# GpSimd in place of VectorE for the gain product of the second token block at the end of the expert stage

## The chip, the core and the metric

The kernel is one program on one core of a Trainium2 chip. The core has TensorE (matrix products into PSUM, abbreviated PE; PEld is its loading of weights), VectorE (DVE), ScalarE (ACT), GpSimd (POOL), SyncE (SP), which issues most DMAs, and 16 DMA engines. All engines run their own instruction lists in order and wait for one another by semaphores. The metric is the time of one execution on the device in microseconds (us); smaller is better.

## What is computed

256 tokens of 1024 features (f32) go through two transformer blocks. The first has a chunkwise mLSTM beside sliding-window attention, cross attention to a memory of 256 rows, and a mixture with product keys (PEER): for each token and each of 8 heads 16 of 16384 experts, each a row of `expert_down` and one of `expert_up`. The second has gated linear attention beside block attention, an MLP of width 4096 and a gated addition of per-layer features. The change lies where the one passes into the other:

```python
def rmsnorm(x, g):
    xf = x.astype(jnp.float32)
    y = xf * lax.rsqrt(jnp.mean(xf * xf, axis=-1, keepdims=True) + EPS)
    return (y * g.astype(jnp.float32)).astype(x.dtype)
...
def first_block(...):
    ...
        h = h + peer_ffn(rmsnorm(h, g_ffn[l]), w_pq[l], sub_keys1[l], sub_keys2[l],
                         expert_down[l], expert_up[l])
    return rmsnorm(h, g_final)
...
def second_block(x, ...):
    ...
        h = rms_norm(x, norm_mix[i])
        u = h @ w_in[i]
        (gq, gk, gv, g_lr, g_r, mq, mk, mv, gate_a, gate_b) = jnp.split(u, points, axis=-1)
```

So the residual stream h after the experts is normed with `g_final`, which gives the second block's input x, and x is normed once more with `norm_mix` and multiplied with the weights `w_in`.

## The kernel before

**Tiling.** The tokens are two blocks of 128 (tb = 0, 1), one token in each of the 128 partitions. `X[:, tb, :]` is the residual stream, 128x1024 f32. Weights come as halves of 128x2048 f32 in a fixed order (`HALVES`) into a ring of three buffers. Each half is cut into two parts for the matrix products: ScalarE copies it rounded into the first tensor of a pair hl (L1439), and VectorE subtracts that from the ring's tile into the second (L2006, one instruction of 2.29 us with two SBUF inputs). On both engines `split_to(n)` does this for all halves up to number n that aren't done. TensorE makes three products for each pair of tiles (L817).

**The expert stage.** 256 indirect DMAs of GpSimd (L781) each gather, for one expert slot of one token block, the down row and the up row of the expert of each of the 128 tokens, into one of 8 buffers. VectorE multiplies and sums the down half of a gathered buffer with the normed tokens XG (L2490, two SBUF inputs of 128x1024), ScalarE applies the gelu (L1695), VectorE the gate (L2498), ScalarE makes a diagonal of the coefficients (L1702) and TensorE adds diagonal times up half to the accumulators in PSUM (L1169). Its last product is semaphore `pe["ex", 255]`. In GpSimd's list a wait for it and two memsets of the scan mask `scanm` (L786, L788) stand behind the gathers; the only reader of the mask is the scan of VectorE at L2529.

**The seam to the second block**, for each token block: VectorE adds the two accumulators to X (`residual_sum`, L2424, semaphore h3). It multiplies X by the factors of `g_final`, which lie in all partitions of GB, into HG (`gain_sum`, L2429, semaphore hgs); HG is the tile XG, whose reader, the expert stage, is done with that block by then. ScalarE squares and sums X (`final_sum`, L1718) and HG (`final_gained`, L1722). From the two sums come both norms: VectorE makes the variances (`final_var`, L2434 to L2437), ScalarE the root (`sqrt`, L1456), VectorE the inverse roots and a diagonal matrix `xdg` with their product (`final_root`, L2442 to L2449). TensorE multiplies HG with this diagonal, which turns and scales it (`turn_block`, L1157, waits for hgs and for the diagonal), ScalarE and VectorE copy the result in two parts to XT (`final_turned`, L1729, L2460), and VectorE writes the plain final norm back to X (`final_scale`, L2452).

For tb = 0 these steps are spread over the last 16 gathers of the second token block. For tb = 1 they stand behind all of them, woven with the halves n to n+3 of the weights of gv (n is the number of gv's first half). VectorE's order there is: split n, `residual_sum(1)`, `gain_sum(1)`, split n+1, `final_var(1)`, `final_root(1)`, split n+2, `final_turned(1)`, `final_scale(1)`. ScalarE's is: splits to n+1, `final_sum(1)`, `final_gained(1)`, two fetches (one loads other factors into GB), split n+2, the root, `final_turned(1)`. TensorE's is: 12 products with half n and 12 with half n+1 for token block 0, the two `turn_block(1, k)`, then 36 more products, the first 12 with half n+2.

Of the kernel before, what the change touches and what calls it, by code (L numbers as in the profile page):

```python
# [11 lines left out]
ALU = mybir.AluOpType  # L12
# [54 lines left out]
def program(nc, A, out):  # L67
    ctx = ExitStack()
    with ctx:
        def sb(name, shape, dt=F32):  # L70
            return ctx.enter_context(nc.sbuf_tensor(name, shape, dt))

        def count(name, keys, by=1):
            return Count(ctx.enter_context(nc.semaphore(name)), keys, by)

        def landed(name):
            return (ctx.enter_context(nc.semaphore(name)), 16)
# [3 lines left out]
        X = sb("X", [128, 2, 1024])  # L81
# [6 lines left out]
        GB = sb("GB", [128, 1024])  # L88
# [94 lines left out]
        HG = XG  # L183
# [51 lines left out]
        for j in range(4):  # L235
# [14 lines left out]
        at = {n: landed(f"c_{n}") for n in ("x0", "x1", "gains", "convw", "convb", "bif", "sinks", "gmh", "sk", "thin",  # L250
                                            "mem", "gb2", "bqk", "gffn", "gfin", "ggn", "gw2", "pT", "wple")}
# [106 lines left out]
        h3 = count("h3", [(tb, h) for tb in range(2) for h in range(2)])  # L358
        hgs = count("hgs", range(2))
# [349 lines left out]
        @block.sync  # L709
        def _(e):  # L710
            for tb in range(2):
                e.dma_start(X[:, tb, :], A["x"][tb * 128:tb * 128 + 128, :]).then_inc(at[f"x{tb}"][0], 16)
            for n, (name, k, h) in enumerate(HALVES):
                if (name, k, h) == ("xv", 0, 0):
                    e.dma_start(PWB[:, :], A["wple"]).then_inc(at["wple"][0], 16)
                    e.dma_start(pT[:, :, :], A["pT"]).then_inc(at["pT"][0], 16)
                if name == "ple":
                    continue
                if n >= RING:
                    e.wait_ge(*lo[n - RING])  # L720
                if n in (NUM["gv", 0, 0], NUM["gv", 0, 1]):
                    e.wait_ge(*gath[254 + n - NUM["gv", 0, 0]])
                e.dma_start(ring[:, n % RING, :], A["wt"][FIRST[name] + 2 * k + h]).then_inc(ld[n][0], 16)
            for k, tb, o, n in LAST:
                c = slice(k * 512 + o, k * 512 + o + n)
                e.wait_ge(*pgo[k, tb, o, n])
                e.dma_start(out[tb * 128:tb * 128 + 128, c], SG[:, tb, c]).then_inc(outs.sem, 16)
            e.wait_ge(*outs[4])


        @block.gpsimd
        def _(e):
            e.memset(ident[:, :], 0.0).then_inc(gstep.sem)
            e.memset(epsc[:, :], EPS)
            e.memset(sel[:, :, :], 0.0)
            e.memset(M1[:, :], 0.0)
            e.memset(CT[:, :], 0.0)
            e.memset(ones[:, :], 1.0)
            e.memset(cmask[:, :], 1.0).then_inc(gstep.sem)
            e.wait_ge(*gstep[0])  # L740
            e.affine_select(out=ident[:, :], in_=ident[:, :], compare_op=ALU.not_equal, fill=1.0, base=0,
                            pattern=[[-1, 128]], channel_multiplier=1).then_inc(const.sem)
            e.wait_ge(*gstep[1])
            e.affine_select(out=sel[:, :, :], in_=sel[:, :, :], compare_op=ALU.not_equal, fill=1.0, base=0,
                            pattern=[[-1, 4], [0, 128]], channel_multiplier=1)
            e.affine_select(out=M1[:, 0:128], in_=M1[:, 0:128], compare_op=ALU.is_gt, fill=NEG, base=0,
                            pattern=[[1, 128]], channel_multiplier=-1)
            e.affine_select(out=M1[:, 128:256], in_=M1[:, 128:256], compare_op=ALU.is_ge, fill=NEG, base=0,
                            pattern=[[-1, 128]], channel_multiplier=1)
            e.affine_select(out=CT[:, :], in_=CT[:, :], compare_op=ALU.is_ge, fill=-NEG, base=0,  # L750
                            pattern=[[1, 128]], channel_multiplier=-1)
            e.iota(ioi, pattern=[[1, 256]], base=-128, channel_multiplier=-1).then_inc(gstep.sem)
            e.wait_ge(*gstep[2])
            e.tensor_copy(DD[:, :], ioi).then_inc(gstep.sem)
            e.wait_ge(*gstep[3])
            e.affine_select(out=DD[:, :], in_=DD[:, :], compare_op=ALU.is_ge, fill=NEG, base=128,
                            pattern=[[-1, 256]], channel_multiplier=1)
            e.iota(ioi[:, 0:16], pattern=[[1, 16]], base=0, channel_multiplier=0).then_inc(gstep.sem)
            e.wait_ge(*gstep[4])
            e.tensor_copy(iot[:, :], ioi[:, 0:16]).then_inc(gstep.sem)  # L760
            e.wait_ge(*gstep[5])
            e.affine_select(out=cmask[0:64, :], in_=cmask[0:64, :], compare_op=ALU.is_ge, fill=0.0, base=0,
                            pattern=[[1, 64]], channel_multiplier=-1).then_inc(gstep.sem)
            e.wait_ge(*gstep[6])
            e.affine_select(out=cmask[64:128, :], in_=cmask[64:128, :], compare_op=ALU.is_ge, fill=0.0, base=0,
                            pattern=[[1, 64]], channel_multiplier=-1).then_inc(const.sem)

            e.wait_ge(*pe["XV", 3])
            for i in range(256):
                h, tb, s = i // 32, i // 16 % 2, 16 * (i // 32) + i % 16  # L770
                if i == 0:
                    e.wait_ge(*idx[0, 0, 0])
                if i == 8 or i % 16 == 0 and i > 0:
                    e.wait_ge(*idx[h, tb])
                if i == 2:
                    e.wait_ge(*pe["xo", 1, 1])
                if i == 6:
                    e.wait_ge(*pe["pq", 0, 1])
                if i >= NG:
                    e.wait_ge(*pe["ex", i - NG])  # L780
                e.indirect_dma_start(out=rows[i % NG][:, :], out_offset=None, in_=A["ex"],  # L781
                                     in_offset=bass.IndirectOffsetOnAxis(ap=eidx[:, tb, s:s + 1], axis=0)
                                     ).then_inc(gath[i][0], 16)

            e.wait_ge(*pe["ex", 255])
            e.memset(scanm, 1.0).then_inc(scan1.sem)  # L786
            e.wait_ge(*scan1[0])
            e.memset(scanm.rearrange("p (a b) -> p a b", b=64)[:, :, 0:1], 0.0).then_inc(scan1.sem)  # L788
# [3 lines left out]
        def _(e):  # L792
# [608 lines left out]
            for h in range(2):  # L1401
                n = NUM["pg", 1, h]
                e.wait_ge(*lo[n])
                w = [p[:, :].rearrange("p (k n) -> p k n", k=4) for p in PARTS[n]]
                for i, (_, tb, o, c) in enumerate(LAST[2:]):
                    ps = bank(("pg", 1, i)) if h == 0 else ps_of(("pg", 1, i))
                    m = prod(ps[:, 0:c], lambda a, k: XT[a][:, k, tb * 128:tb * 128 + 128],
                             lambda b, k: w[b][:, k % 4, o:o + c], range(4 * h, 4 * h + 4), h == 0, h == 1)
                    if h:
                        mark(m, ("pg", 1, i))  # L1410
                if h == 0:
                    mark(m, ("used", n))
# [572 lines left out]
        def _(e):  # L1985
# [13 lines left out]
            def split_to(n):  # L1999

                while parted[0] <= min(n, len(HALVES) - 1):
                    i = parted[0]
                    parted[0] += 1
                    e.wait_ge(*hi[i])
                    w = PARTS[i]
                    e.tensor_tensor(w[1][:, :], loaded(i), w[0][:, :].bitcast(F32),  # L2006
                                    ALU.subtract).then_inc(lo.sem)
# [412 lines left out]
            def residual_sum(tb):  # L2420
                e.wait_ge(*pe["ex", 239 + 16 * tb])
                for h in range(2):
                    x = X[:, tb, h * 512:h * 512 + 512]
                    e.tensor_tensor(x, ps_of(("acc", tb, h))[:, :], x, ALU.add).then_inc(h3.sem)  # L2424

            def gain_sum(tb):
                e.wait_ge(*at["gfin"])
                e.wait_ge(*h3[tb, 1])
                e.tensor_tensor(HG[:, tb, :], X[:, tb, :], GB[:, :], ALU.mult).then_inc(hgs.sem)  # L2429
# [84 lines left out]
            n = NUM["gv", 0, 0]  # L2514
            split_to(n)
            residual_sum(1)
            gain_sum(1)
            split_to(n + 1)
            final_var(1)
            final_root(1)  # L2520
# [286 lines left out]
```

## Time and profile before

| what | value |
| --- | --- |
| median of 3 runs | 1406.13 us (1404.08 to 1406.48) |
| the profiled execution | 1404.8 us |
| its span, first to last instruction | 1403.0 us |
| TensorE busy | 1265.9 us (90%) |
| VectorE busy | 947.8 us (68%) |
| ScalarE busy | 585.7 us (42%) |
| GpSimd busy | 273.8 us (20%) |

A page of the profile gives one execution. Times are counted from the start of the span. A timeline row has the start in us, the busy time in us, the engine, the line of the kernel, the operation, the tiles written and read (without buffer numbers: B is any of the working tiles, HG, the row buffers and the scan mask among them; st is a tile of small sums), the shapes and the number of instructions that the row merges. In brackets stands how long the engine had been idle before, and what ended this. The chain that ended last is followed backwards from the last instruction, each step to what released it. Of the engines' busy times the highest share isn't the answer by itself: what counts at one place is which wait ends last there.

### The profile page before, as it was taken

Reading aid. Unit: us, or ns where it says so; the run is one execution under the profiler, and the core shown is the slowest. Engines: PE = TensorE matmul, PEld = TensorE weight load, DVE = VectorE, ACT = ScalarE, POOL = GpSimd, SP = SyncE. Lnnn points to the kernel's source line nnn. Section 1 sums busy time; section 2 is a strip of 40 time slices with the busy share of each in tenths; the row PEclk is TensorE's granted clock in tenths of the full one; section 3 lists DMA queues with packets and bytes.
Section 4 is the critical chain, followed back from the end, with each engine's and each line's share of the span. In section 5 each row is a group of like instructions: output and inputs, shape, how many; then the busy total and the mean of one; then the engine's idle time right before and its main releaser. Section 6 shows DMA issues by size and latency. Waiting matters only on the chain.

```text
span 1403.0 us, 15322 instructions
## 1 busy us (share of the span) xinstructions
PE 1265.9 (90%) x5502; PEld 869.3 (62%) x5502; DVE 947.8 (68%) x1973; ACT 585.7 (42%) x1045; POOL 273.8 (20%) x281
## 2 busy tenths in 40 slices
PE   8999998988788878878787779899999999999998
PEld 8888897544243333424343234388688878888887
DVE  5657656877777777777777776655765556877445
ACT  4657453322223232222322223565556644555334
POOL 1000001443334344343434345100000000000000
PEclk9999998799999999999999999999999999999999
DMA  7443533999999999999999999845354445455551
GB/s 285 169 169 111 183 113 145 413 421 421 421 421 421 421 422 418 422 410 421 419 422 421 421 415 413 337 163 196 121 180 150 150 155 186 170 193 197 184 205 61
DMA packets 57123, 398.73 MB, mean 284 GB/s; under 512 B 7112, under 2 KB 7624, under 8 KB 9176
## 3 DMA queue, kind: packets, MB, share of 16 engines
q0 software_dynamic: 36864, 268.45, 46.2%
q1 hardware_dynamic: 18144, 126.10, 25.1%
q10 hardware_dynamic: 2040, 3.19, 0.7%
q8 instruction: 45, 0.74, 0.2%
q14 instruction: 30, 0.25, 0.0%
HBM read 396.67 MB, written 1.05 MB: 283 GB/s over the span
## 4 chain that ended last, share of the span: by engine, by line
PE 56%; DMA 24%; DVE 8%; ACT 7%; issue 3%; POOL 0%; ACTq 0%; SPq 0%; DVEq 0%; POOLq 0%
PE ps L817 35%; DMA B<-in_ex,eidx 23%; PE ps L1169 10%; PE ps L845 4%; DVE B L2490 3%; ACT hl L1439 3%; PE ps L846 2%; DVE hl L2006 2%; ACT diags L1702 1%; DMA ring<-in_wt 1%; ACT av_ L1695 1%; ACT L1695 1%; ACT L1691 1%; PE ps L1067 0%; PE ps L1049 0%
## 5 line engine op out<-in xcount | busy, mean ns | idle before, releaser
L1169 PE MATMUL ps<-B,diags 128*128 128x512 f32 x1024 | 487.9, 622 | 114.7 <-ACT diags L1702 114.7
L1169 PEld LDWEIGHTS ps<-B,diags 128*128 128x128 f32 x1024 | 191.3, 196 | 382.2 <-issue 197.0
L2490 DVE CUSTOM_DVE_ANT_0 B<-B 128x1024 f32<-128x1024 f32 x256 | 311.4, 1221 | 118.5 <-DMA B<-in_ex,eidx 118.4
L781 POOL DMA_INDIRECT B<-in_ex,eidx x256 | 267.7, 1046 | 611.8 <-PE ps L1169 363.8
L2006 DVE TENSOR_TENSOR hl<-ring,hl 128x2048 fp32r<-128x2048 f32 x115 | 263.2, 2290 | 180.0 <-ACT hl L1439 179.7
L1439 ACT ACTIVATE hl<-ring 128x2048 fp32r<-128x2048 f32 x115 | 219.8, 1912 | 117.5 <-PE ps L817 116.0
L817 PE MATMUL ps<-hl,R 128*128 128x512 f32 x936 | 218.2, 392 | 0.3 <-DVE R L2022 0.3
L817 PE MATMUL ps<-hl,XT 128*128 128x512 f32 (+1 forms) x888 | 203.6, 387 | 2.9 <-DVE hl L2006 2.4
L1695 ACT ACTIVATE av_<-av_ 128x2 f32<-128x2 f32 x128 | 26.0, 203 | 426.5 <-DVE av_ L2490 426.4
L817 PEld LDWEIGHTS ps<-hl,R 128*128 128x128 f32 x936 | 174.2, 188 | 36.8 <-DVE R L2022 0.7
L817 PEld LDWEIGHTS ps<-hl,XT 128*128 128x128 f32 x888 | 162.4, 188 | 38.6 <-DVE hl L2006 3.7
L817 PE MATMUL ps<-XT,hl 128*128 128x256 f32 x960 | 133.7, 297 | 2.9 <-DVE XT L2015 2.9
L817 PEld LDWEIGHTS ps<-XT,hl 128*128 128x128 f32 x960 | 120.9, 193 | 17.0 <-issue 16.4
L1702 ACT ACTIVATE diags<-ident,av_ 128x128 f32<-128x128 f32 x256 | 88.8, 394 | 29.1 <-DVE av_ L2498 29.1
L845 PE MATMUL ps<-XT,hl 128*128 128x512 f32 x256 | 89.1, 392 | 0.0
L846 PE MATMUL ps<-XT,hl 128*128 128x256 f32 x256 | 71.7, 280 | 0.0
L845 PEld LDWEIGHTS ps<-XT,hl 128*128 128x128 f32 x256 | 47.9, 187 | 10.8 <-DVE XT L2015 0.3
L2498 DVE TENSOR_TENSOR av_<-av_,gw 128x2 f32<-128x2 f32 x128 | 20.7, 162 | 43.9 <-ACT av_ L1695 43.8
L846 PEld LDWEIGHTS ps<-XT,hl 128*128 128x128 f32 x256 | 48.4, 189 | 0.0
L1959 ACT ACTIVATE B<-ps 128x256 f32<-128x256 f32 x32 | 10.5, 381 | 37.2 <-PE ps L846 37.2
L817 PE MATMUL ps<-R,hl 128*128 128x256 f32 x192 | 24.4, 286 | 0.4 <-DVE R L2015 0.4
L817 PEld LDWEIGHTS ps<-R,hl 128*128 128x128 f32 x192 | 23.4, 192 | 1.4 <-issue 0.7
(362 smaller groups left out, 990.0 us busy)
## 6 DMA issues: line engine op xcount, KB each, us to landing
ring<-in_wt SPq DMA_DIRECT2D x117, 1024.0 KB, 4.8
B<-in_ex,eidx POOLq DMA_INDIRECT x256, 13.4
X<-in_x SPq DMA_DIRECT2D x2, 512.0 KB, 4.6
B<-in_mem ACTq DMA_DIRECT2D x1, 1024.0 KB, 10.6
PW<-in_wple SPq DMA_DIRECT2D x1, 1024.0 KB, 7.2
out<-B SPq DMA_DIRECT2D x3, 256.0 KB, 2.0
GB<-in_gffn ACTq DMA_DIRECT2D x1, 512.0 KB, 3.9
GB<-in_gfin ACTq DMA_DIRECT2D x1, 512.0 KB, 9.2
```

Source lines behind the costliest of these rows:

```text
L781: e.indirect_dma_start(out=rows[i % NG][:, :], out_offset=None, in_=A["ex"], in_offset=bass.IndirectOffsetOnAxis(ap=eidx[:, tb, s:s + 1], ...
L817: m = e.matmul(ps, lhs(a, k), rhs(b, k), start=start and (a, b, k) == (0, 0, ks[0]), stop=stop and (a, b, k) == (1, 0, ks[-1]))
L845: e.matmul(y, w[0][:, i, c * 128:c * 128 + 128], XTT[:, :, i, :], start=i == 0, stop=False)
L846: m = e.matmul(y[:, 0, :], w[1][:, i, c * 128:c * 128 + 128], XT[0][:, i, :], start=False, stop=i == 7)
L1169: m = e.matmul(acc[tb][hf][:, :], diags[:, i % 4, :], rows[i % NG][:, 1024 + 512 * hf:1536 + 512 * hf], start=(s == 0), stop=(s == 127))
L1439: e.activation(PARTS[i][0][:, :], loaded(i), ACT.Copy).then_inc(hi.sem)
L1691: e.activation(gj, gj, ACT.Exp, accum_out=smx[:, 0:1]).then_inc(gexp.sem)
L1695: e.activation(av_[:, tb, s:s + 2], av_[:, tb, s:s + 2], ACT.Gelu).then_inc(gelu.sem)
L1702: e.activation(diags[:, (i + z) % 4, :], ident[:, :], ACT.Copy, scale=av_[:, tb, s + z:s + z + 1]).then_inc(dgx.sem)
L2006: e.tensor_tensor(w[1][:, :], loaded(i), w[0][:, :].bitcast(F32), ALU.subtract).then_inc(lo.sem)
L2490: m = e.tensor_tensor_reduce(R[:, 0:1024], R[:, 0:1024], XG[:, tb, :], 1.0, 0.0, ALU.mult, ALU.add, av_[:, tb, s + z:s + z + 1])
L2498: e.tensor_tensor(av_[:, tb, s:s + 2], av_[:, tb, s:s + 2], gw[:, tb, s:s + 2], ALU.mult).then_inc(coef.sem)
```

## The change

GpSimd's list gets three instructions between the last gather and the memsets: a wait for the factors in GB, a wait for the second residual sum of block 1, and the multiply, which raises the same semaphore hgs. VectorE's call of `gain_sum(1)` is taken out; that for block 0 stays on VectorE.

```diff
@@ -781,6 +781,10 @@
                 e.indirect_dma_start(out=rows[i % NG][:, :], out_offset=None, in_=A["ex"],
                                      in_offset=bass.IndirectOffsetOnAxis(ap=eidx[:, tb, s:s + 1], axis=0)
                                      ).then_inc(gath[i][0], 16)
+
+            e.wait_ge(*at["gfin"])
+            e.wait_ge(*h3[1, 1])
+            e.tensor_tensor(HG[:, 1, :], X[:, 1, :], GB[:, :], ALU.mult).then_inc(hgs.sem)
 
             e.wait_ge(*pe["ex", 255])
             e.memset(scanm, 1.0).then_inc(scan1.sem)
@@ -2514,7 +2518,6 @@
             n = NUM["gv", 0, 0]
             split_to(n)
             residual_sum(1)
-            gain_sum(1)
             split_to(n + 1)
             final_var(1)
             final_root(1)
```

## Rows read from the trace of the kernel before

**Rows 1.** The page, the chain that ended last: share of the span by engine.

```profile
PE 56%; DMA 24%; DVE 8%; ACT 7%; issue 3%; POOL 0%; ACTq 0%; SPq 0%; DVEq 0%; POOLq 0%
```

**Rows 2.** The chain in order of time, 880 to 1000 us: start, us, what.

```profile
901.45 1.92 ACT hl L1439
...
908.21 2.21 DVE hl L2006
...
915.27 13.79 PE ps L817 x72
```

**Rows 3.** Timeline of VectorE, 897 to 950 us: start, us, instruction, idle before.

```profile
903.39 2.29 DVE L2006 TENSOR_TENSOR hl<-ring,hl 128x2048 fp32r<-128x2048 f32 x1 [2.77 <-ACT hl L1439]
905.60 1.28 DVE L2424 TENSOR_TENSOR X<-ps,X 128x512 f32<-128x512 f32 x2
906.99 1.23 DVE L2429 TENSOR_TENSOR B<-X,GB 128x1024 f32<-128x1024 f32 x1
908.13 2.29 DVE L2006 TENSOR_TENSOR hl<-ring,hl 128x2048 fp32r<-128x2048 f32 x1
...
912.56 0.29 DVE L2449 TENSOR_SCALAR B<-ident,st 128x128 f32<-128x128 f32 x1
912.76 2.29 DVE L2006 TENSOR_TENSOR hl<-ring,hl 128x2048 fp32r<-128x2048 f32 x1
...
939.66 2.29 DVE L2529 TENSOR_TENSOR_SCAN B<-B 128x1024 f32<-128x1024 f32 x1
```

**Rows 4.** Timeline of ScalarE, 897 to 950 us.

```profile
907.27 1.05 ACT L1718 ACTIVATE B<-X 128x1024 f32<-128x1024 f32 x1
...
908.31 1.04 ACT L1722 ACTIVATE B<-B 128x1024 f32<-128x1024 f32 x1
...
911.15 0.19 ACT L1456 ACTIVATE st<-st 128x2 f32<-128x2 f32 x1
```

**Rows 5.** Timeline of TensorE, 897 to 950 us.

```profile
910.47 3.02 PE L817 MATMUL ps<-hl,XT 128*128 128x512 f32 x12 [1.71 <-DVE hl L2006]
913.33 1.95 PE L1157 MATMUL ps<-B 128*128 128x128 f32 x16
915.10 8.45 PE L817 MATMUL ps<-hl,XT 128*128 128x512 f32 x36
```

**Rows 6.** Timeline of GpSimd, the start and 897 to 950 us.

```profile
4.17 0.40 POOL L754 CAST DD<-B 128x256 f32<-128x256 int32 x1
...
5.28 0.20 POOL L760 CAST iot<-B 128x16 f32<-128x16 int32 x1
...
905.07 0.95 POOL L786 MEMSET B<- 128x1024 f32 x1 [19.50 <-PE ps L1169]
```

**Rows 7.** Timelines of VectorE and GpSimd, 250 to 300 and 866 to 880 us.

```profile
251.87 2.28 DVE L2006 TENSOR_TENSOR hl<-ring,hl 128x2048 fp32r<-128x2048 f32 x1
...
252.37 2.60 POOL L781 DMA_INDIRECT B<-in_ex,eidx  x1 [6.26 <-PE ps L817]
...
873.21 1.23 DVE L2490 CUSTOM_DVE_ANT_0 B<-B 128x1024 f32<-128x1024 f32 x1 [1.00 <-DMA B<-in_ex,eidx]
...
873.26 1.98 POOL L781 DMA_INDIRECT B<-in_ex,eidx  x1 [1.39 <-PE ps L1169]
...
878.08 0.94 POOL L781 DMA_INDIRECT B<-in_ex,eidx  x1 [1.60 <-PE ps L1169]
```

**Rows 8.** Windows: stretch, length, busy us by engine, PEclk, DMA share, GB/s.

```profile
13.20:16.00 2.80, 0.00 (x0) 0.01 (x1) 1.00 (x3) 1.87 (x6) 0.00 (x0) 1.00 0.87 273
16.20:19.50 3.30, 3.25 (x15) 2.95 (x15) 2.54 (x7) 3.30 (x5) 0.00 (x0) 0.50 1.01 397
...
894.20:896.10 1.90, 0.00 (x0) 0.00 (x0) 1.63 (x5) 0.58 (x3) 0.00 (x0) 1.00 0.08 34
896.90:900.20 3.30, 3.30 (x5) 1.24 (x5) 2.20 (x4) 0.00 (x0) 0.00 (x0) 0.50 0.78 276
...
910.50:913.90 3.40, 3.40 (x18) 2.90 (x19) 2.80 (x11) 0.84 (x2) 0.00 (x0) 1.00 0.87 296
```

## The prediction

> **What bounds the kernel now.** I read the chain that ended last first. By the page it is 56% TensorE and 24% DMA [rows 1], and the DMA part belongs to the expert rows. So I asked where the changed instruction stands in it. In order of time the chain leaves the weights' DMA at 901.45 us and then passes through the block that the diff touches, with VectorE's split of the next weight half, before it stays with TensorE [rows 2]. From 915.27 us the chain is TensorE's products for a long way, with engines that only follow them; no DMA stands in it there, so a delay of TensorE at 915 us is carried to the end, and nothing later is fixed in time that could swallow it. The question is thus by how much the start of TensorE's 36 products at 915.10 us moves.
>
> Then I laid the timelines of the engines side by side. VectorE: residual sums of the second block, 905.60 to 906.89; the multiply in question (L2429), 1.23 us from 906.99; the split of half n+1 (the second of the gv weights), 2.29 us from 908.13; the small steps of the final norm; the diagonal (L2449) from 912.56 to 912.85; the split of half n+2, 912.76 to 915.05 [rows 3]. ScalarE: square of X until 908.3, square of HG (L1722) from 908.31, then its own part of half n+2, and the root at 911.15 [rows 4]. TensorE: 12 products of gv, a wait of 1.71 us, 12 more from 910.47, the turning at 913.33, and the 36 products at 915.10, 0.05 us behind the end of VectorE's split [rows 3, 5]. So three strands meet at 913 to 915 us. The one through the product HG runs: HG, square on ScalarE, ScalarE's part of n+2, root, VectorE's last norm steps, the diagonal, VectorE's split of n+2, TensorE. It has no slack to speak of.
>
> **What is removed.** VectorE no longer spends 1.23 us on L2429. Its split of n+1 follows the residual sums directly. Back to back instructions overlap by 0.08 us here (908.13 against 906.99 + 1.23 = 908.22), so it runs from 906.81 to 909.10 instead of 908.13 to 910.42. TensorE's second group of 12 products starts at 909.15 or a little later instead of 910.47, and ends near 912.2. This gain of 1.3 us is worth nothing: the next thing TensorE needs is the diagonal, and that hangs on HG.
>
> **What is added.** One multiply of 128x1024 f32 with two SBUF inputs on GpSimd, which waits for the gains (landed long before) and for the second residual sum. GpSimd has issued its last gather by then and had stood idle for 19.5 us at 905.07. Behind the new wait in its queue stand only the two memsets of the scan mask, the first of which ran at 905.07 [rows 6]; they move to about 911.3 us, and the scan that reads them starts at 939.66 [rows 3]. This cover of over 27 us makes them free. Nothing else is moved past a queue; no DMA is added.
>
> **How long GpSimd takes.** No two-input operation of GpSimd is in the trace. Nearest rows: its cast takes 0.40 us for 256 columns and 0.20 us for 16, so 0.83 ns a column, and 0.20 + 1008 x 0.83 ns = 1.04 us for 1024 columns with one input; a memset of 1024 columns, which only writes, takes 0.95 us [rows 6]. So reading and writing overlap, and a pass costs 0.83 ns a column. One pass (1.04 us) is the lower bound; three passes that don't overlap (0.2 + 3 x 0.85 = 2.75 us) the upper. Two reads through what serves one input at a pace of one pass each give 1.9 us, and the third pass is hidden at best. I take 2.2 us, an estimate between two passes and three, nearer to the two. The Trainium skill (GPSIMD Engine Reference, Elementwise — side-by-side cycle accounting) measures 4497 ns for a two-input add of 2048 f32 columns, and explains it by two operands that share one read port; half of it, an estimate, is 2.25 us, and by it the sum below would be 0.05 us larger. No row here shows such an operation.
>
> **When GpSimd may start.** This is the term that decides. VectorE's split of n+1 also has two SBUF inputs (ring and hl). The rows of the gathers show what such an instruction does to GpSimd: a gather issue that starts at 873.26, 0.05 us behind a two-input VectorE operation of 873.21 to 874.44, takes 1.98 us instead of 0.94 and ends 0.80 us behind VectorE's end; another starts at 252.37 inside a VectorE split that ends at 254.15, takes 2.60 us and ends 0.82 us behind it [rows 7]. An issue that nobody hinders takes 0.94 us, as at 878.08. Of the 44 gather issues that began inside such a VectorE operation, 43 (the two shown are the first and the last of them) ended 0.80 to 0.82 us behind its end; the one that did not had begun only 0.03 us after it. As the bare issue is 0.94 us, GpSimd's work goes on 0.13 us before VectorE's recorded end. Here VectorE starts its split at 906.81, before the residual sum has even signalled (906.89), so it is at least 0.1 us ahead of GpSimd. GpSimd is held until 908.97, and HG is ready at 908.97 + 2.2 = 911.17. The Trainium skill (SBUF — State Buffer, SBUF: two separate sides) says that a VectorE operation with two SBUF inputs and a GpSimd operation that reads SBUF exclude each other for a whole instruction, and that the first to start wins; these rows agree with it.
>
> **The sum.** ScalarE starts the square of HG at 911.17 + 0.10 = 911.27 instead of 908.31 (the 0.10 us is what lies between the end of L2429 and that start) [rows 3, 4]. That is 3.0 us later. Everything behind keeps its distances: root 2.84 us after that start (911.15 - 908.31), now held by ScalarE's part of n+2 alone, at 914.1; diagonal done at 915.8; split of n+2 done at 918.0; TensorE's 36 products at 918.1, not 915.10. The turning starts at 915.8 and ends 1.95 us later, at 917.8, just before. Hence +3.0 us; with 1.04 or 2.75 us for GpSimd it would be +1.8 or +3.5.
>
> **The clock on top.** TensorE now idles from about 912.2 to 915.8 us, 3.6 us. That is longer than any of its waits in the trace behind the first microseconds; they reach 2.9 us. Two of them are in the rows: behind one of 2.9 us (13.15 to 16.02) the granted clock is 0.50, the 1.2 GHz level, for 3.3 us, and the same follows one of 2.0 us (894.20 to 896.17), while the 1.71 us before 910.47 are followed by the full 2.4 GHz [rows 5, 8]. Of the 16 waits of at least 1.9 us, of which these two are the first and the last, 12 were followed by the half clock, and none of the shorter ones. So I expect such a stretch here too. 3.3 us at half speed cost at most 1.65 us; part of them falls before 918.1 us, where TensorE waits anyway or is only turning, and costs little. Between 0.6 (half of it covered, the turning stretched past VectorE's split) and 1.6, I take 1.1 us. The forecast is +3.0 + 1.1 = +4.1 us.
>
> **Against the times.** The profiled execution took 1404.8 us, with a span of 1403.0; by the sum it would take 1404.8 + 4.1 = 1408.9. The median of the three runs is 1406.13, 1.3 above it. I add the change to the median: 1406.1 + 4.1 = 1410.2 us.
>
> **The rivals.**
> - Hold, but no clock stretch: +3.0, 1409.1 us. For it: 4 of the 16 long waits had none.
> - GpSimd dearer than I take it (three passes or a start-up of its own): +3.5 with the clock's 1.1 gives +4.6 or more, 1410.7 to 1412. Against a start-up: its memset at 905.07 followed 256 gathers at the usual pace.
> - No hold, so the result is not slower by what can be measured: GpSimd works beside the split from 906.95 to 909.15, ScalarE starts at 909.25, +0.95 us, TensorE idles only 1.5 us at the seam, the clock stays: 1407.1 us. It decides if GpSimd's access is not of the kind that the gathers use. For it: the memset at 905.07 ran beside the split of 903.39 to 905.68 at its usual pace, but it reads nothing [rows 3, 6]. Against it: 43 of 44 [rows 7].
> - The other order: GpSimd is first and VectorE's split is held to 909.15 and ends at 911.4; the norm steps follow it 1.0 us late and the root 1.2 us late: about +1.3 us, 1407.4. It needs VectorE to start after GpSimd, against the 0.1 us above.
> - Faster: with one pass and no hold HG would be ready at 908.0, but ScalarE is busy with the square of X until 908.3, and VectorE's freed 1.23 us lie before a wait. So at best nothing is won, about 1406, and only scatter would show a gain.
>
> **How the numbers follow.** Chances: forecast 0.50, hold without clock 0.17, dearer 0.09, no hold 0.13, other order 0.07, nothing or a gain 0.04. What a measurement of this kernel can tell from no change is about 0.2%, 2.8 us. Scatter of the runs is 1404.1 to 1406.5, so +4.1 comes out above 2.8 in nine of ten, +3.0 in six of ten: slower 0.45 + 0.10 + 0.09 = 0.64, same 0.32, faster 0.04. The range runs from just below the no-hold case, 1406.9, to the dear case, 1412.2; it leaves out a tenth at either end.
>
> **What the profile after will show.** GpSimd's multiply recorded from 906.95 with about 4.2 us, ending 2.1 us behind VectorE's split (a record of 2.2 us would mean no hold; a split longer than 2.29 us, the other order). TensorE's second group of 12 products at 909.2; square of HG at 911.3; turning at 915.8; the 36 products at 918.1; a granted clock of 0.50 somewhere in 914 to 921; the memsets behind 911 with nobody waiting. It is wrong above all if the multiply is not held, or takes far from 2.2 us.

## The result: 0.3 to 0.4% slower

Six executions of the changed kernel have a median of 1411.43 us (1409.99 to 1412.37), six of the kernel before 1405.76 us (1404.08 to 1406.48): ratio 1.0042, 95% interval 1.0029 to 1.0055, which is 5.9 us, between 4.1 and 7.7. The profiled execution took 1409.99 us with a span of 1407.8 us, 4.8 more than before. One execution of a later variant (VectorE with one SBUF input) took 2085.9 us at a low granted clock; it is not counted.

Below are the rows that answer to those of before. Lines of the kernel are shifted by 3 or 4: L2010 is the split that was L2006, L2428 the residual sums (L2424), L1726 the square of HG (L1722), L2453 the diagonal (L2449), L1161 the turning (L1157). The whole seam also stands 0.5 us later than before, because the expert stage ended that much later. I come back to that at the end of the experiments; positions are therefore taken from the start of the residual sums, 906.13 here and 905.60 before [rows 3]. From the changed kernel's timelines of VectorE, ScalarE, GpSimd and TensorE, each by time:

```profile
906.13 1.28 DVE L2428 TENSOR_TENSOR X<-ps,X 128x512 f32<-128x512 f32 x2
907.33 2.28 DVE L2010 TENSOR_TENSOR hl<-ring,hl 128x2048 fp32r<-128x2048 f32 x1
...
916.17 0.28 DVE L2453 TENSOR_SCALAR B<-ident,st 128x128 f32<-128x128 f32 x1
916.37 2.28 DVE L2010 TENSOR_TENSOR hl<-ring,hl 128x2048 fp32r<-128x2048 f32 x1
...
944.56 2.29 DVE L2532 TENSOR_TENSOR_SCAN B<-B 128x1024 f32<-128x1024 f32 x1
```

```profile
907.84 1.05 ACT L1722 ACTIVATE B<-X 128x1024 f32<-128x1024 f32 x1
...
911.91 1.06 ACT L1726 ACTIVATE B<-B 128x1024 f32<-128x1024 f32 x1 [2.93 <-POOL B L787]
...
914.76 0.19 ACT L1460 ACTIVATE st<-st 128x2 f32<-128x2 f32 x1
```

```profile
907.57 4.31 POOL L787 TENSOR_TENSOR B<-X,GB 128x1024 f32<-128x1024 f32 x1 [21.44 <-DVE X L2428]
911.83 0.94 POOL L790 MEMSET B<- 128x1024 f32 x1
```

```profile
909.67 3.04 PE L821 MATMUL ps<-hl,XT 128*128 128x512 f32 x12 [0.38 <-DVE hl L2010]
916.60 2.64 PE L1161 MATMUL ps<-B 128*128 128x128 f32 x16 [3.89 <-DVE B L2453]
918.89 9.56 PE L821 MATMUL ps<-hl,XT 128*128 128x512 f32 x36
928.28 2.94 PE L821 MATMUL ps<-XT,thin 128*16 128x256 f32 x24
```

Read them from GpSimd's row. The multiply is recorded for 4.31 us, and ends at 911.88, 2.27 us behind VectorE's split (907.33 + 2.28 = 909.61). ScalarE had idled 2.93 us for it and starts the square of HG 5.78 us behind the residual sums, where it was 2.71 [rows 4]. The diagonal comes 10.04 us behind them instead of 6.96 [rows 3]. TensorE began its second group of 12 products 1.3 us early and then waited 3.89 us for the diagonal. Last, the 36 products take 9.56 us where they took 8.45 [rows 5]: the clock. In the windows of the changed kernel (stretch, length, busy time and count of PE, PEld, DVE, ACT and POOL, granted clock, DMA share, GB/s) the wait and the half clock behind it are plain:

```profile
912.70:916.60 3.90, 0.01 (x2) 0.03 (x1) 2.04 (x12) 2.25 (x4) 0.20 (x2) 1.00 0.62 252
917.60:920.60 3.00, 3.00 (x14) 2.71 (x13) 2.33 (x6) 2.29 (x8) 0.00 (x0) 0.54 0.30 63
921.20:928.20 7.00, 7.00 (x32) 5.74 (x31) 1.47 (x4) 2.38 (x2) 0.00 (x0) 1.00 0.22 90
```

And GpSimd, at 0% of the chain before [rows 1], is now a link of it. The page's line, and two pieces of the chain in order of time:

```profile
PE 55%; DMA 25%; DVE 8%; ACT 8%; issue 3%; POOL 1%; ACTq 0%; SPq 0%; DVEq 0%; POOLq 0%
```

```profile
907.57 4.32 POOL B L787
...
919.23 14.73 PE ps L821 x72
```

To compare kernels I use one figure of each trace, the length of the seam: from the start of the residual sums to the start of TensorE's 24 thin products behind the 36. Before it is 923.39 - 905.60 = 17.79 us, with 923.39 from TensorE's timeline, which had this row:

```profile
923.39 2.94 PE L817 MATMUL ps<-XT,thin 128*16 128x256 f32 x24
```

In the changed kernel it is 928.28 - 906.13 = 22.15 us. The seam has become 4.36 us longer. With the start 0.5 us later, that is the whole difference of the two traces: behind the seam 479.6 us are left before and 479.5 after (spans 1403.0 and 1407.8).

### The profile page after: what moved, and what is told of

It is laid out like the page before. It is cut to its first block, busy times and chain, and to the rows that moved or that the text cites. A ratio compares the mean times of both kernels' runs of the same rounds, so it can differ in the third digit from the quotient of the medians.

```text
span 1407.8 us, 15322 instructions
## 1 busy us (share of the span) xinstructions
PE 1266.0 (90%) x5502; PEld 870.5 (62%) x5502; DVE 946.6 (67%) x1972; ACT 586.1 (42%) x1045; POOL 278.9 (20%) x282
## 3 DMA queue, kind: packets, MB, share of 16 engines
q10 hardware_dynamic: 2040, 3.19, 0.7%
## 4 chain that ended last, share of the span: by engine, by line
PE 55%; DMA 25%; DVE 8%; ACT 8%; issue 3%; POOL 1%; ACTq 0%; SPq 0%; DVEq 0%; POOLq 0%
PE ps L821 34%; DMA B<-in_ex,eidx 24%; PE ps L1173 10%; PE ps L849 4%; DVE B L2494 3%; ACT hl L1443 3%; PE ps L850 2%; DVE hl L2010 1%; ACT diags L1706 1%; DMA ring<-in_wt 1%; ACT L1695 1%; ACT av_ L1699 1%; PE ps L1071 0%; PE ps L1053 0%; POOL B L781 0%
## 5 line engine op out<-in xcount | busy, mean ns | idle before, releaser
L2010 DVE TENSOR_TENSOR hl<-ring,hl 128x2048 fp32r<-128x2048 f32 x115 | 263.2, 2290 | 181.3 <-ACT hl L1443 181.1
```

## The experiments

My theory (A) was the one of the prediction: VectorE's split holds GpSimd back, GpSimd then takes twice VectorE's time, HG is late by the sum, and the long wait of TensorE costs a stretch of half clock on top. The rivals: a two-input multiply of GpSimd takes 4.3 us by itself; the clock is not part of it; something outside the seam costs as well. Times below are the ratio to the kernel before, timed beside each variant on the same chip, with its 95% interval, turned into us. Where I count "behind the residual sums", it is from their start; the recorded expectations count it from their end, 1.28 us later.

**The changed kernel again.** No edit.

> The changed kernel once more, to measure the whole change beside the other variants. In its profile the seam (TensorE's 36 products of gv, start and end against the residual sums of VectorE) costs 3.1 us by the late product HG and 1.1 us by a stretch of half clock. Theory A (these two are all): 4.4 us over the kernel before, single executions between 3.1 and 4.8 by where the half clock falls. Theory B (something outside the seam costs as well, since the medians stood 5.7 us apart): 5.7 us again, with about 1.3 us of it to be found outside 905 to 928 us.

Measured: ratio 1.0034 (1.0022 to 1.0046), +4.8 us, between 3.1 and 6.5; medians 1411.12 against 1406.22. Its seam is 927.83 - 905.71 = 22.12 us, +4.33. The first timing's surplus over the seam (1.5 us by the ratio, 1.3 by the medians) did not come back; what is left, 0.5 us, is inside the interval. The traces speak against theory B: behind the seam 479.6 us are left in this one, as in the kernel before. A surplus in other executions can't be ruled out by that.

**VectorE's split waits for the multiply.**

```diff
             residual_sum(1)
+            e.wait_ge(*hgs[1])
             split_to(n + 1)
```

> As the changed kernel, but VectorE's split of half n+1 waits until GpSimd's multiply is done. If VectorE's two-input split held GpSimd back (theory A), the multiply's record falls from 4.3 to 2.2 to 2.5 us, HG is ready about 2.45 us behind the residual sums, the split ends 4.7 us behind them, and the norm is late by 1.3 us only: +1.3 us over the kernel before without a half clock, up to +2.8 with one (TensorE now waits 3 us before its second group). If a two-input multiply of GpSimd simply takes 4.3 us (rival), the record stays 4.3 us, the split ends 6.6 us behind the residual sums and the time is +3.5 us or more, as slow as the changed kernel.

GpSimd's, VectorE's and TensorE's timelines of this variant:

```profile
907.01 2.38 POOL L787 TENSOR_TENSOR B<-X,GB 128x1024 f32<-128x1024 f32 x1 [21.46 <-DVE X L2428]
```

```profile
905.58 1.28 DVE L2428 TENSOR_TENSOR X<-ps,X 128x512 f32<-128x512 f32 x2
909.42 2.29 DVE L2010 TENSOR_TENSOR hl<-ring,hl 128x2048 fp32r<-128x2048 f32 x1 [2.57 <-POOL B L787]
...
913.82 0.29 DVE L2453 TENSOR_SCALAR B<-ident,st 128x128 f32<-128x128 f32 x1
```

```profile
911.77 4.60 PE L821 MATMUL ps<-hl,XT 128*128 128x512 f32 x12 [3.03 <-DVE hl L2010]
916.21 1.95 PE L1161 MATMUL ps<-B 128*128 128x128 f32 x16
```

The record is 2.38 us once the split is out of the way: a multiply of GpSimd does not take 4.3 us. The diagonal is 8.24 us behind the residual sums, 1.28 later than before, as worked out. The clock struck at another place: TensorE waited 3.03 us ahead of its second group, which then took 4.60 us instead of 3.02. Seam +2.81 us; measured +2.2 us (1.0 to 3.4).

**TensorE kept busy while it waits.** In TensorE's list, ahead of the turning of block 1:

```diff
+            e.wait_ge(*h3[0, 1])
+            w = [p[:, :].rearrange("p (k n) -> p k n", k=4) for p in PARTS[n]]
+            for i in range(14):
+                e.matmul(ps_of(("x2T", 1, 0))[:, :], XT[0][:, i % 4, 0:128], w[0][:, i % 4, :], start=True, stop=True)
             for k in range(2):
                 turn_block(1, k)
```

> As the changed kernel, but TensorE makes 14 idle products of 128x512 (3.3 us, into a bank that the turning overwrites) while it waits for the diagonal. They add work that nothing needs. If the half clock behind the long wait costs what the profile suggests (theory A), the granted clock stays 1.00 from 908 to 925 us and the time falls by 0.6 to 1.6 us against the changed kernel, to about +3.1 us over the kernel before. If the clock is not part of the loss (rival), the time is that of the changed kernel, or more where the idle products run into the turning.

TensorE's timeline of this variant, and a window over the turning and what follows:

```profile
910.83 3.33 PE L1196 MATMUL ps<-hl,XT 128*128 128x512 f32 x14
914.86 2.02 PE L1161 MATMUL ps<-B 128*128 128x128 f32 x16 [0.70 <-DVE B L2457]
916.97 8.46 PE L821 MATMUL ps<-hl,XT 128*128 128x512 f32 x36
```

```profile
914.90:918.00 3.10, 3.02 (x20) 2.65 (x21) 2.81 (x5) 1.97 (x8) 0.00 (x0) 1.00 0.17 26
```

Fourteen products for nobody made the kernel faster than without them: full clock throughout, 8.46 us for the 36 products, seam +3.08 us (925.27 - 904.40 = 20.87), measured +3.1 us (1.8 to 4.4). The multiply's record stayed 4.30 us. On another chip, beside a later variant:

> The changed kernel with 14 idle products of TensorE once more, on this chip, beside the other: +3.1 us over the kernel before, and 1.8 us more than the variant in which VectorE's split waits and TensorE's gap is filled too. This difference is the hold alone (GpSimd's multiply ends 2.27 us behind the split, which takes 2.28, against 2.38 us behind the residual sums).

Seam +3.12 us, measured +3.4 us (2.1 to 4.6). So by the seams the half clock is worth 1.2 to 1.3 us of the changed kernel's 4.4, and the rest, 3.1, is HG's lateness. The timings alone, with intervals 2.5 us wide, would not tell the two variants apart from the changed kernel.

**Another operation of VectorE beside the multiply.** The low part of half n+1 is left out (zeros), and VectorE reads one SBUF input at a time:

```diff
-            split_to(n + 1)
...
+            e.wait_ge(*hi[i])
+            e.tensor_reduce(rsq[:, 0:1], loaded(i), AX, ALU.add)
+            e.tensor_scalar(PARTS[i][1][:, :], loaded(i), 0.0, None, ALU.mult).then_inc(lo.sem)
```

> As the changed kernel, but in place of VectorE's split of half n+1 (two SBUF inputs, 2.3 us) stand a sum over the same 128x2048 elements (one SBUF input, about 2.2 us) and then a multiply by zero into the low part; so the low parts of that half of the gv weights are left out of the result. If only two-input operations of VectorE hold GpSimd (theory A), the multiply runs beside the sum and its record is 2.2 to 2.5 us; HG is 2.45 us behind the residual sums and the time is about +1.2 us over the kernel before. If any operation of VectorE on SBUF holds it, the record stays near 4.3 us and the time near +3.1 to +4.4 us.

VectorE's and GpSimd's timelines of it:

```profile
906.60 2.27 DVE L2525 TENSOR_REDUCE st<-ring 128x1 f32<-128x2048 f32 x1
908.79 2.39 DVE L2526 TENSOR_SCALAR hl<-ring 128x2048 fp32r<-128x2048 f32 x1
```

```profile
906.84 2.38 POOL L787 TENSOR_TENSOR B<-X,GB 128x1024 f32<-128x1024 f32 x1 [21.41 <-DVE X L2428]
909.16 0.94 POOL L790 MEMSET B<- 128x1024 f32 x1
910.17 1.09 POOL L792 MEMSET B<- 128x16 f32 x1
```

TensorE's:

```profile
911.24 4.61 PE L821 MATMUL ps<-hl,XT 128*128 128x512 f32 x12 [2.70 <-DVE hl L2526]
```

The sum over the same 2048 columns, as long as the split and begun 0.24 us ahead of the multiply, does not hold it: 2.38 us, as alone. So it is not enough that VectorE is busy on SBUF. But the sum differs from the split in two ways: it reads one SBUF tile instead of two, and it writes one column instead of 2048. The trace of the kernel before has a case that tells these apart, for gather issues. Timelines of VectorE and GpSimd, 864 to 867 us:

```profile
865.10 1.29 DVE L2424 TENSOR_TENSOR X<-ps,X 128x512 f32<-128x512 f32 x2
865.64 0.93 POOL L781 DMA_INDIRECT B<-in_ex,eidx  x1 [0.30 <-issue]
```

The residual sum of block 0 writes 1024 columns to SBUF, and one of its two inputs lies in PSUM; the issue begun inside it takes 0.93 us, as alone. An issue begun inside the gain product of block 0 (869.84 to 871.07), which writes as many columns and reads two SBUF tiles, takes 1.28 us. So it is what VectorE reads: two SBUF inputs hold, one in these two operations does not. This is what the Trainium skill states (SBUF — State Buffer, SBUF: two separate sides), and here the hold is shown for a multiply, not only for gather issues. Seam +2.49 us, of which the clock took about 1.6 (the second group needed 4.61 us), which my expectation had left out; measured +1.4 us (0.0 to 2.7).

**The memsets first.** They go back ahead of the multiply in GpSimd's list.

> As the changed kernel, but the two memsets of the scan mask stand ahead of GpSimd's multiply, where they ran before the change (0.95 and 0.13 us from the end of the expert stage, done 0.8 us before the residual sums). Theory A: the queue order is without effect, the multiply starts 0.1 us behind the residual sums as before and its record stays 4.3 us; +4.8 us over the kernel before, as measured for the changed kernel in the same way. Rival: the moved memsets are part of the loss; then the time falls by up to 1 us and the scan or another reader shows it.

GpSimd's timeline:

```profile
904.98 0.95 POOL L786 MEMSET B<- 128x1024 f32 x1 [19.49 <-PE ps L1173]
905.99 0.13 POOL L788 MEMSET B<- 128x16 f32 x1
907.17 4.29 POOL L792 TENSOR_TENSOR B<-X,GB 128x1024 f32<-128x1024 f32 x1 [1.06 <-DVE X L2428]
```

The same multiply, held as before. Seam +4.32 us, measured +4.2 us (2.5 to 5.9). The place in the queue plays no part in the seam.

**VectorE makes HG itself, but late.** The kernel before, with two calls exchanged:

```diff
             residual_sum(1)
-            gain_sum(1)
             split_to(n + 1)
+            gain_sum(1)
```

> The kernel before with VectorE's two instructions exchanged: split of half n+1 first, then VectorE's own multiply (1.23 us), and no GpSimd. It makes HG late by the split's place alone. Theory A (only the time at which HG is ready matters, whoever makes it): HG ready 3.35 us behind the residual sums and the square of HG 2.0 us later than before; TensorE waits about 2.6 us for the diagonal, so a half clock is likely; +2.0 us without it, up to +3.5 with it. Rival (GpSimd itself costs something beyond the lateness of HG): +1 us or less.

VectorE's multiply, the square and the turning (timelines of three engines):

```profile
909.09 1.22 DVE L2429 TENSOR_TENSOR B<-X,GB 128x1024 f32<-128x1024 f32 x1
```

```profile
910.34 1.06 ACT L1722 ACTIVATE B<-B 128x1024 f32<-128x1024 f32 x1 [1.85 <-DVE B L2429]
```

```profile
915.04 3.19 PE L1157 MATMUL ps<-B 128*128 128x128 f32 x16 [2.80 <-DVE B L2449]
```

The square starts 4.64 us behind the residual sums (905.70), 1.93 later than before; the wait of 2.80 us brought a half clock, with which the turning took 3.19 us. Seam +3.24 us, measured +2.1 us (0.8 to 3.5). No GpSimd in the seam, and the same kind of loss: the diagonal is 1.95 us late, the clock adds 1.3. What counts is when HG is ready.

**Two multiplies on GpSimd.** The first writes to a tile that nobody reads.

```diff
+            e.tensor_tensor(Bf[10][:, 0:1024], X[:, 1, :], GB[:, :], ALU.mult)
             e.tensor_tensor(HG[:, 1, :], X[:, 1, :], GB[:, :], ALU.mult).then_inc(hgs.sem)
```

> As the changed kernel, but GpSimd multiplies twice, first into a tile that nobody reads. Theory A (the multiply is held until the split ends, then takes 2.4 us, and every us of it is on the path): the first record 4.3 us, the second 2.35 us, HG and the diagonal 2.35 us later than in the changed kernel, +7.2 us over the kernel before, up to 0.5 us more if half clock falls on more of TensorE's work. Rival (some other wait ends last at the diagonal, so that GpSimd has slack): less than +6 us.

GpSimd's timeline:

```profile
907.35 4.30 POOL L787 TENSOR_TENSOR B<-X,GB 128x1024 f32<-128x1024 f32 x1 [21.46 <-DVE X L2429]
911.62 2.35 POOL L788 TENSOR_TENSOR B<-X,GB 128x1024 f32<-128x1024 f32 x1
```

In one list: 4.30 us held, 2.35 us not held. The diagonal comes 2.30 us later than in the changed kernel (918.26 - 905.92 = 12.34), TensorE waits 6.18 us and works longer at half clock, so that the seam grows by more than the second multiply. Seam +7.70 us, measured +6.6 us (4.5 to 8.7, from three executions); the medians differ by 7.1. There is no slack on this path.

**Half on each engine.** VectorE multiplies columns 0 to 511 ahead of its split, GpSimd the rest; the square and the turning wait for both.

> As the changed kernel, but GpSimd multiplies only the columns 512 to 1023 and VectorE the columns 0 to 511 ahead of its split of half n+1. Both are ready to start within 0.1 us. GpSimd's part takes about 1.2 us alone (half of 2.38). Theory A1: VectorE's half (0.68 us) goes first, GpSimd gets in between it and the split; its record is about 1.8 us, the split is held and ends 4.3 us behind the residual sums instead of 2.2: about +0.9 us over the kernel before. Theory A2: VectorE's next instruction follows without a gap and GpSimd is held over both; its record is about 4 us, HG ready 4.1 us behind the residual sums: about +2.8 us plus the clock.

The timelines of VectorE and then of GpSimd:

```profile
908.22 0.69 DVE L2527 TENSOR_TENSOR B<-X,GB 128x512 f32<-128x512 f32 x1
908.83 3.39 DVE L2015 TENSOR_TENSOR hl<-ring,hl 128x2048 fp32r<-128x2048 f32 x1
```

```profile
908.34 1.73 POOL L788 TENSOR_TENSOR B<-X,GB 128x512 f32<-128x512 f32 x1 [21.53 <-DVE X L2433]
```

GpSimd, begun 0.12 us behind VectorE's half, is held by it and then gets in ahead of the split, although that starts without a gap. Now it is the split that is held: 3.39 us instead of 2.28. So the hold works in both directions. HG is ready 0.5 us later than before, the seam is +0.94 us, measured +1.7 us (0.4 to 3.0). The other 0.4 us of the seam is ScalarE's, whose second fetch took 0.95 us here (0.45 before), so that its part of half n+2 began late:

```profile
910.48 0.95 ACTq L1449 DMA_DIRECT2D B<-in_gw  x1
...
911.53 1.91 ACT L1446 ACTIVATE hl<-ring 128x2048 fp32r<-128x2048 f32 x1 [0.28 <-issue]
```

Why that fetch was slower was not tried. TensorE's longest wait in this seam was 2.19 us, ahead of its second group, and no half clock followed.

**GpSimd alone, and TensorE kept busy.** The variant with the waiting split, plus 11 idle products ahead of TensorE's second group.

> The variant in which VectorE's split of half n+1 waits for GpSimd's multiply, and in which TensorE makes 11 idle products (2.6 us, into a bank that the turning overwrites) while it waits for that split. Neither the hold nor a long wait of TensorE is left, only GpSimd's 2.38 us against VectorE's 1.23. Theory A: granted clock 1.00 from 905 to 925 us, the diagonal 1.25 us later than in the kernel before, TensorE's second group of 12 products 1.3 us later, +1.2 to +1.4 us over the kernel before. Rival (GpSimd's part in the seam costs something that the clock and the hold do not explain): +2 us or more, as the variant without the idle products.

TensorE's timeline:

```profile
912.10 3.04 PE L821 MATMUL ps<-hl,XT 128*128 128x512 f32 x12 [0.54 <-DVE hl L2014]
914.98 1.95 PE L1161 MATMUL ps<-B 128*128 128x128 f32 x16
916.69 8.46 PE L821 MATMUL ps<-hl,XT 128*128 128x512 f32 x36
```

Full clock, no long wait. Seam +1.30 us (924.98 - 905.89 = 19.09), measured +1.8 us (0.6 to 3.1). Against the changed kernel with its gap filled (+3.1) the seam is 1.8 us shorter; that is what the hold costs. The timing alone would also allow the rival's 2 us; the seam does not. By the records of the multiply alone the hold is 1.93 us (4.31 against 2.38) and GpSimd's slowness 1.15 us (2.38 against 1.23). The 1.3 us of this variant hold about 0.1 us more, because with the split so late ScalarE's root waits for VectorE's variances.

The account of the seam's 4.36 us is thus: 1.3 us because GpSimd is slower than VectorE, 1.8 us because VectorE's split goes first and holds it, 1.2 to 1.3 us of half clock. All of the eleven timings contain the length of their seam in their intervals. No variant was faster than the kernel before: where VectorE's time was freed, it lay ahead of a wait.

What lies outside the seam scatters by itself. The residual sums start anywhere from 904.40 to 906.90 us in the traces. And behind the seam 479.5 or 479.6 us are left in eight of the twelve traces but 481.1 or 481.2 in four (the waiting split, the memsets first, half on each engine, GpSimd alone and filled): in these four, TensorE's products of L845 and L846 (line numbers of before) took 91.0 us from first to last, in the others 89.4. The memsets-first variant has it and the changed kernel does not, though the two differ in the memsets alone; its cause stays open. That is why I rest on the seams, and take from the timings only that they agree.

## Why the prediction was right

- **What bounds the seam.** Right. The strand through HG had no slack: with TensorE's gap filled, a diagonal later by 3.07 us made the seam longer by 3.1 us at full clock.
- **What is removed.** Right. The split starts 1.20 us behind the start of the residual sums (1.21 worked out), TensorE's second group early, at no gain. (The overlap of instructions back to back is 0.09 us by the rows cited, not 0.08.)
- **GpSimd's price.** The mechanism was right, the term a little small: 2.38 us measured alone, 2.2 taken; the bounds 1.04 and 2.75 held it. The estimate from the Trainium skill (GPSIMD Engine Reference, Elementwise — side-by-side cycle accounting), 2.25 us, was nearer.
- **The hold.** Right, from gather issues alone: 4.31 us recorded, about 4.2 forecast, 2.27 us behind the split instead of 2.1. The count of 44 issues was stated too broadly: it holds for those that began more than 0.13 us ahead of the end of VectorE's two-input operation. 96 more began in its last 0.13 us, and 95 of them took their bare 0.93 to 0.95 us. That fits the reading that GpSimd goes on 0.13 us before VectorE's recorded end, and changes nothing for a split of which nearly all lay ahead. Together HG's lateness is 3.07 us at the square (5.78 - 2.71), against 3.0.
- **The clock.** Right that it would come. Its price was 1.29 us, 0.18 in the turning and 1.11 in the products, against 1.1. With it the wait that ended last ahead of the 36 products changed, as the lower case of the range (0.6) had it: they started 0.24 us behind the end of VectorE's split of n+2 (918.65), when the turning, stretched by the half clock, made way. The 1.1 was a choice between 0.6 and 1.6, so that it came this close is partly luck.
- **The sum.** +4.36 us in the trace, against +4.1. The first median stood 5.7 us above that of before, and 1.2 us above the forecast of 1410.2; the second timing gave +4.9 between medians, and the variant with the memsets first, whose seam is the same, +5.0. All three stand above 4.1; of this the seam explains 0.26 us, and the rest is no larger than the scatter outside the seam.
- **The rivals.** No hold (+0.95) and the other order (+1.3) did not occur here; half on each engine showed the other order is real once GpSimd gets in first. By the median alone, 1411.43 us, the dearer GpSimd (1410.7 to 1412) would fit better than the forecast; the traces decide against it, with 2.38 us where it needs 2.75. Nor does a start-up show: 2.38 us for a multiply after 21 us of idleness, 2.35 us for one right behind another. That there would be a half clock at all was no certainty: 4 of 16 long waits before had none.
- **The memsets.** Free, as said: the first ended at 912.77, the scan came at 944.56.

## What to carry to other kernels

Before moving an elementwise operation to an idle GpSimd, look at what VectorE does at that moment: an instruction with two SBUF inputs held GpSimd's multiply and its gather issues until it ended, and the freed engine may start just such an instruction at once. Then ask what the freed time is worth; here it lay ahead of a wait, while the moved operation lay on the path. And where a new wait of TensorE exceeds those that were followed by half clock in the old trace, count on the clock in its price: it was more than a quarter of this loss.

## What the runs showed of the hardware beyond that

- Products that nobody needs paid for themselves: 3.3 us of them in a 3.9 us wait of TensorE took 1.2 us off the seam (22.12 and 22.15 us without them, 20.87 and 20.91 with).
- Half clock followed waits of 2.70, 2.80, 3.03, 3.89, 3.91 and 6.18 us at the seam, and none of 2.19 us or less there. That is no limit: in the expert stage just before it, the wait of 1.94 to 1.98 us that every trace has (894.20 to 896.17 before) was followed by half clock in eight of the twelve traces and not in the other four, and in the kernel before one of 2.88 us (516.57 to 519.44) was not. So the length of a wait alone does not decide it. Behind the wait of 6.18 us it cost most: the diagonal was 5.38 us late (12.34 - 6.96) and the seam 7.70 us longer, so 2.3 us against the 1.3 of the changed kernel.
- VectorE's multiply by a constant (L2526 above) took 2.39 us for 2048 columns, though `final_scale` (also a multiply by a scalar) takes 0.74 us for 1024; it had begun 0.4 us before GpSimd's multiply ended. GpSimd's memset of 16 columns took 1.09 us instead of 0.13 and ended 0.08 us behind it. So this kind of VectorE instruction, with one SBUF input, seems to wait for GpSimd and to hold even its writes: two SBUF inputs may not be the only thing that holds. That was seen in passing and not tried by itself.
